# Segment sums of a Mamba-2 scan as split float32r products, and a reordered mixer stage

## What is computed

```
Acs = jnp.cumsum(dtc * A.reshape(G, E), axis=2)
seg = Acs[:, :, :, None] - Acs[:, :, None, :]
Lmat = jnp.exp(jnp.where(causal, seg, -jnp.inf))
y_diag = jnp.einsum('bcign,bcjgn,bcijge,bcjgep->bcigep', CB, Lmat, xdt)
log_a = -LRU_C * r * jax.nn.softplus(-lam)      # r, ig: sigmoids of two small products
u = jnp.sqrt(-jnp.expm1(2.0 * log_a)) * (ig * xf)
_, h = lax.associative_scan(_lin_combine, (jnp.exp(log_a), u), axis=1)
lru_out = rmsnorm(h * jax.nn.gelu(lru_y), lru_out_norm)
```

## Time and profile before

| | before |
|---|---|
| median of 3 runs | 2287.84 us (2287.51 to 2288.26) |
| profiled execution | 2287.8 us, of which the span is 2286.1 us |
| granted clock of TensorE, mean | 0.996 |
| PE busy | 2245.0 us (98%) in 14337 matmul records |
| VectorE, ScalarE, GpSimd busy | 994.8 us (44%), 474.2 us (21%), 745.6 us (33%) |
| chain that ended last | PE 93%, DVE 2%, ACT 2%, DMA 1%, issue 1% |

### The profile page before, as it was taken

How to read it: one execution, slowest core, us unless ns; L and a number is a source line. 1 busy time by engine, 2 the same in 40 slices (tenths; PEclk the granted TensorE clock), 3 DMA queues, 4 the chain that set the end, 5 groups by cost and what they waited for, 6 DMA issues and landing times.

```text
span 2286.1 us, 32012 instructions
## 1 busy us (share of the span) xinstructions
PE 2245.0 (98%) x14337; PEld 2195.3 (96%) x14337; DVE 994.8 (44%) x792; ACT 474.2 (21%) x601; POOL 745.6 (33%) x415
## 2 busy tenths in 40 slices
PE   8999999999999999999999999999999999999997
PEld 8999999999999999988888999999999999999997
DVE  6422122311233557857677586773231123212336
ACT  4100000000002225465564540120000001000102
POOL 4333333333333223432523642323333333333340
PEclk9999999999999999999999999999999999999999
DMA  4111111111112422310111422111111111111112
GB/s 150 47 47 47 47 47 47 47 47 47 47 42 79 130 75 93 121 41 30 49 39 36 170 75 86 47 47 47 47 47 47 47 47 47 46 47 47 47 56 75
DMA packets 48456, 138.35 MB, mean 61 GB/s; under 512 B 7608, under 2 KB 16312, under 8 KB 48320
## 3 DMA queue, kind: packets, MB, share of 16 engines
q1 hardware_dynamic: 47168, 135.78, 18.6%
q10 hardware_dynamic: 1152, 0.52, 0.1%
HBM read 117.67 MB, written 18.79 MB: 60 GB/s over the span
## 4 chain that ended last, share of the span: by engine, by line
PE 93%; DVE 2%; ACT 2%; DMA 1%; issue 1%; ACTq 0%; SPq 0%; POOL 0%; DVEq 0%; POOLq 0%
PE set L572 85%; PE set L807 2%; ACT gate_x L934 1%; PE set L738 1%; PE pair L705 1%; PE set L705 1%; PE pair L713 1%; ACT gate_a L934 1%; PE set L592 0%; PE set L753 0%; PE set L689 0%; PE set L731 0%; PE pair L731 0%; PE pair L735 0%; PE set L735 0%
## 5 line engine op out<-in xcount | busy, mean ns | idle before, releaser
L461 POOL TENSOR_SCALAR w_hi<-w_raw 128x1024 fp32r<-128x1024 f32 (+1 forms) x181 | 193.1, 1067 | 1431.7 <-PE set L572 1230.6
L463 POOL TENSOR_TENSOR w_lo<-w_raw,w_hi 128x1024 fp32r<-128x1024 f32 (+1 forms) x181 | 451.5, 2494 | 27.3 <-issue 0.9
L572 PE MATMUL set<-x_lo,w_hi 128*128 128x344 f32 x2112 | 448.9, 321 | 3.7 <-DVE x_lo L1110 3.7
L572 PE MATMUL set<-x_hi,w_hi 128*128 128x344 f32 x2112 | 449.2, 321 | 1.1 <-ACT x_hi L850 1.1
L572 PE MATMUL set<-x_hi,w_lo 128*128 128x344 f32 x2112 | 446.4, 320 | 0.0
L572 PEld LDWEIGHTS set<-x_lo,w_hi 128*128 128x128 f32 x2112 | 357.8, 189 | 4.6 <-DVE x_lo L1110 4.6
L572 PEld LDWEIGHTS set<-x_hi,w_hi 128*128 128x128 f32 x2112 | 355.7, 188 | 2.2 <-POOL w_lo L470 1.3
L572 PEld LDWEIGHTS set<-x_hi,w_lo 128*128 128x128 f32 x2112 | 352.3, 188 | 0.0
L1106 DVE TENSOR_TENSOR up<-set,rstd 128x1032 f32<-128x1032 f32 x43 | 53.0, 1233 | 419.8 <-PE set L572 419.8
L572 PE MATMUL set<-u_hi,w_hi 128*128 128x344 f32 x864 | 199.1, 339 | 5.4 <-POOL w_lo L463 5.0
L572 PE MATMUL set<-h_hi,w_hi 128*128 128x344 f32 x948 | 201.2, 321 | 0.8 <-DVE h_lo L1130 0.8
(11 more groups left out here) (260 smaller groups left out, 2579.7 us busy)
## 6 DMA issues: line engine op xcount, KB each, us to landing
w_raw<-in_gate_up SPq DMA_DIRECT2D x87, 512.0 KB, 3.5
w_raw<-in_w_in SPq DMA_DIRECT2D x36, 512.0 KB, 4.3
w_raw<-in_down SPq DMA_DIRECT2D x32, 512.0 KB, 3.5
w_raw<-in_w_out SPq DMA_DIRECT2D x16, 512.0 KB, 3.9
w_raw<-in_down SPq DMA_DIRECT2D x16, 384.0 KB, 3.2
x<-in_xt SPq DMA_DIRECT2D x8, 516.0 KB, 8.5
x_kept<-x SPq DMA_DIRECT2D x8, 516.0 KB, 5.0
mixed<-power SPq DMA_DIRECT2D x8, 516.0 KB, 2.9
```

The source lines that it names most:

```text
L461: pool.tensor_scalar(w_hi[s][:, 0:n], w_raw[s][:, 0:n], 1.0, 0.0, ALU.mult, ALU.add)
L463: pool.tensor_tensor(w_lo[s][:, 0:n], w_raw[s][:, 0:n], w_hi[s][:, 0:n].bitcast(F32), ALU.subtract).then_inc(split, 1)
L572: end = pe.matmul(out[:, c, 0:CH], w[s][:, k * P:(k + 1) * P], x[:, kx, c * CH:(c + 1) * CH], start=(first and n == 0), stop=(last and n = ...
```

## The change

- **Segment sums.** In chunks 1 to 7 the product runs in float32r on two terms, `seg_high` and `seg_low`, against a float32r copy `later_r`: four matmuls of 512 columns for each half where there were two in float32. `a` is split once into `a_hi` and `a_lo` (in the storage of `dtw`). ScalarE makes `seg_high` in 16 copies of 128x128 with a scale for each head, at the end of its slot; GpSimd makes `seg_low` in two operations of 1024 columns. Chunk 0 stays as it was.
- **High weights.** ScalarE makes `w_hi` of lx(1) to lx(7); GpSimd makes the low part alone.
- **Waits.** `turn` waits for the first increment of `gate_read` of its slot, which covers `set1`; the second is waited for in `seg(0)`.
- **ScalarE's order.** `btok` comes ahead of the decay terms; both `lmat` exponentials ahead of the root; then the first tap, `e2` and GELU, the high weights and high terms.
- **VectorE's order.** The input of the scan is formed after the second mask; the convolution is in two parts around the first `skip_and_state`. `outputs(1)` stands ahead of tile 2 of ly instead of tile 3.
- **After the slots.** The loads of z2 and z3 are issued ahead of `z_back` and of the prompt state; z2 is scaled ahead of the last scan; the sums "ssd0" and "ssd1" move from z7 to ol2 and from ol3 to ol4, with their roots and reciprocals.

```diff
@@ sync
+            load(("z", EARLY))
+            load(("z", EARLY + 1))
+            sp.wait_ge(state_read, 2 * NCH)
+            for n in range(EARLY):
+                sp.wait_ge(z_stored[n], 16)
+                sp.dma_start(z_back[n][:], d.z_kept[n]).then_inc(z_landed, 16)
+            sp.dma_start(d.prompt_state, ...)
             for t in range(EARLY, KT):
-                load(("z", t))
+                if t >= EARLY + 2:
+                    load(("z", t))
...
@@ gpsimd, split_unit
+                if name[0] == "lx" and name[1]:
+                    pool.wait_ge(lx_high, name[1])
+                else:
...
@@ gpsimd, slots
-                    seg_terms(c + 1)
+                    for g in range(GROUPS):
+                        mine = a_lo[:, c + 1, g * GH:(g + 1) * GH].bitcast(F32)
+                        pool.tensor_tensor(segr_lo[g][:], tri[:].unsqueeze(1).broadcast_to([P, GH, QC]),
+                                           mine.unsqueeze(2).broadcast_to([P, GH, QC]), ALU.mult).then_inc(segr_low, 1)
@@ tensor, turn and seg
-                        pe.wait_ge(gate_read, 2 * c)
+                        pe.wait_ge(gate_read, 2 * c - 1)
...
                         pe.wait_ge(segr_ready, c + 1)
+                        if c:
+                            pe.wait_ge(gate_read, 2 * c)
+                    if c:
+                        pe.wait_ge(segr_low, 2 * c - 1 + g)
...
+                        for low, part in enumerate((segr_hi[:, h:h + 4, :], segr_lo[g][:, 4 * n:4 * n + 4, :])):
+                            end = pe.matmul(to, later_r[:], part.rearrange("p h t -> p (h t)"),
+                                            start=(low == 0), stop=(low == 1))
...
-                products(("ly", c), u_hi, u_lo, {3: lambda: outputs(1)})
+                products(("ly", c), u_hi, u_lo, {2: lambda: outputs(1)})
@@ scalar
+            def seg_terms(c):
+                act.wait_ge(seg_done, 2 * c)
+                act.wait_ge(a_split, 1)
+                for h in range(HEADS):
+                    last = act.activation(segr_hi[:, h, :], tri[:], ACT.Copy, scale=a_hi[:, c, h:h + 1].bitcast(F32))
+                last.then_inc(segr_ready, 1)
...
+                    lru_gelu(c - 1)
+                if c < NCH - 1:
+                    u = U(("lx", c + 1))
+                    act.wait_ge(used, u - 1)
+                    act.wait_ge(landed[u % 2], 16 * (u // 2 + 1))
+                    act.activation(w_hi[u % 2][:], w_raw[u % 2][:], ACT.Copy).then_inc(lx_high, 1)
+                    seg_terms(c + 1)
@@ vector
                 mask(c, 1)
+                if c:
+                    lru_scan_input(c - 1)
+                convolve_first(XT + c, lraw[c % 2], lacc)
                 skip_and_state(c, 0)
-                convolve(XT + c, lraw[c % 2], lacc)
+                convolve_rest(XT + c, lraw[c % 2], lacc)
```

More of the change, by code:

```diff
@@ L134, in make_plan @@
         s = 1 - s
-        if t in (4, 7):
-            p.take(("sum", "lru" if t == 4 else "ssd0"), s)
+        if t == 4:
+            p.take(("sum", "lru"), s)
     for m in range(KT):
@@ L139, in make_plan @@
         s = 1 - s
-        if m == 3:
-            p.take(("sum", "ssd1"), s)
+        if m in (2, 4):
+            p.take(("sum", "ssd0" if m == 2 else "ssd1"), s)
     for m in range(KT):
@@ L230, in build @@
         segr = at("seg_terms", Y, [HEADS, QC])
+        segr_hi = at("seg_high", Y, [HEADS, QC], F32R)
+        segr_lo = [at(f"seg_low{g}", Y + 2 + g, [GH, QC], F32R) for g in range(GROUPS)]
         lmat = [at(f"lmat{g}", Y + 2 + g, [GH, QC]) for g in range(GROUPS)]
@@ L411, in sync @@
                     sp.dma_start(d.mixed[:, 6 if t == 2 else 7, :], sq[:]).then_inc(mixed_stored, 16)
-                if t == 2:
-                    sp.wait_ge(state_read, 2 * NCH)
-                    sp.dma_start(d.prompt_state, ht[:].rearrange("p h c -> p (h c)")).then_inc(outputs_stored, 16)
-                    for n in range(EARLY):
-                        sp.wait_ge(z_stored[n], 16)
-                        sp.dma_start(z_back[n][:], d.z_kept[n]).then_inc(z_landed, 16)
                 if t == 5:
@@ L770, in tensor @@
                     pe.wait_ge(gate_read, 2 * NCH)
-                hooks = {4: {4: lambda: sums("lru", tl, KT - 1)}, 7: {6: lambda: sums("ssd0", t0, 3)}}.get(t)
+                hooks = {4: lambda: sums("lru", tl, KT - 1)} if t == 4 else None
                 products(("z", t), u_hi, u_lo, hooks)
             for m in range(KT):
-                products(("ol", m), l_hi, l_lo, {4: lambda: sums("ssd1", t1, 3)} if m == 3 else None,
-                         l_split if m == 0 else None)
+                hooks = {2: {4: lambda: sums("ssd0", t0, 3)}, 4: {4: lambda: sums("ssd1", t1, 3)}}.get(m)
+                products(("ol", m), l_hi, l_lo, hooks, l_split if m == 0 else None)
             pe.wait_ge(s_split, KT)
@@ L996, in scalar @@
                                    ACT.Exp).then_inc(lmat_exp, 1)
-                    if c and g == 0:
-                        lru_finish(c - 1)
+                if c:
+                    lru_root(c - 1)
+                else:
+                    act.wait_ge(dec_y, KT)
+                freed(("lx", c))
+                first_tap(XT + c, lraw[c % 2], lacc)
                 if c:
@@ L1009, in scalar @@
             lru_decays(NCH - 1)
-            lru_finish(NCH - 1)
+            lru_root(NCH - 1)
+            lru_gelu(NCH - 1)
             def z_tile(t):
@@ L1034, in scalar @@
                     root("lru", tl, 1.0 / DM)
-                if t == 7:
-                    root("ssd0", t0, 2.0 / DM)
                 z_tile(t)
@@ L1203, in vector, with tap, convolve_first, convolve_rest @@
             reciprocal("mix", rstd)
-            def convolve(q, raw, acc):
-                dve.wait_ge(tap0, q + 1)
-                for k in range(HIST):
-                    dve.drain()
-                    n = HIST - k
-                    last = dve.scalar_tensor_tensor(acc[:, n:PROMPT], raw[:, 0:PROMPT - n], pars[:, q, k:k + 1],
-                                                    acc[:, n:PROMPT], ALU.mult, ALU.add)
-                    if k == 0:
-                        dve.tensor_tensor(acc[:, PROMPT:T], acc[:, PROMPT:T], hist_sum[:, q, :], ALU.add)
-                last.then_inc(convolved, 1)
+            def tap(q, raw, acc, k):
+                n = HIST - k
+                dve.drain()
+                return dve.scalar_tensor_tensor(acc[:, n:PROMPT], raw[:, 0:PROMPT - n], pars[:, q, k:k + 1],
+                                                acc[:, n:PROMPT], ALU.mult, ALU.add)
+            def convolve_first(q, raw, acc):
+                dve.wait_ge(tap0, q + 1)
+                tap(q, raw, acc, 0)
+                dve.tensor_tensor(acc[:, PROMPT:T], acc[:, PROMPT:T], hist_sum[:, q, :], ALU.add)
+            def convolve_rest(q, raw, acc):
+                tap(q, raw, acc, 1)
+                tap(q, raw, acc, 2).then_inc(convolved, 1)
+            def convolve(q, raw, acc):
+                convolve_first(q, raw, acc)
+                convolve_rest(q, raw, acc)
             def decode_scale(t):
```

65 lines of the change are left out of this document (38 added, 27 removed).

## The result

The changed kernel takes 2257.05 us (median of four runs, 2256.04 to 2258.64) against 2287.68 us (2286.89 to 2288.26) for the kernel before on the same chip. The ratio is 0.9867, with a 95% interval of 0.985 to 0.9884. Forecast were 2255.1 us and a range of 2250 to 2263 us. The profiled execution took 2256.04 us, 2254.3 us of it span, with a mean granted clock of 0.998.

A forecast was written before the change was run, and what follows sets the result against it. TensorE was taken as the bound, busy nearly the whole span, with waits mostly in the mixer. Terms 10.9 + 10.0 + 5.1 - 0.7 + 7.0 + 0.4 = 32.7 us, from 2287.8 to 2255.1 us; range 2250 to 2263 us.

The forecast's parts named there:

- Segment sums: Chunks 1 to 7: four 512-column float32r matmuls take 0.94 us a half instead of 1.72 us; gain 10.9 us.
- z3: Behind the slots: issuing z3's load half a slot earlier ends its wait and the lower clock; gain 7.0 us.
- ol0: Unit ol0: the root's wait goes, a 1.3 us wait at tiles 6 and 7 comes; net gain 0.4 us.
- The turn: Transposes in each slot: the first increment of the gate reading falls before TensorE arrives, so their wait goes; gain 10.0 us.
- Both exponentials first: First outputs in each slot: the second exponential ends at about 13.6 us, so their wait goes; gain 5.1 us.
- The border: Six slot borders: scan and GpSimd's low part exclude each other, holding lx 0.35 us each; net -0.7 us.
- Rival (1): Slot borders: the scan gets in first, TensorE isn't held and 2.1 us come back; 2253.0 us, chance 0.20.
- (2): Slots: a ScalarE or VectorE chain is 2 us longer, each slot loses 1 to 1.5 us; 2262 to 2266 us, chance 0.17.
- (3): z3 still waits, as the new queue puts its load behind a full buffer; 2262.1 us, chance 0.08.
- (4): Segment sums: float32r at 512 columns is no faster than float32; 2266.0 us, chance 0.04.
- (5): Slots: ScalarE becomes the bound through slow float32r copies; about 2292 us at 0.9 us a copy, chance 0.02.
- (6): ScalarE in the slots: a function-set switch also drains for 1.38 us, making e2 late; 2272.5 us, chance 0.03.

The follow-up runs named there:

- the kernel before with the new queue: Kernel before, with loads of z2 and z3, then z_back, the prompt state and the mixed tiles issued in that order behind the slots: 2279.74 us.

## Why the prediction was right, and where not

The three steps in the slots and z3 went by the mechanism that was walked. The term that failed is ol0, a small gain by the forecast and a loss in the runs; beside it the border came out better than forecast, and the edit named for z3 is not the one that was needed.

**Segment sums**, forecast 10.9 us: 0.92 us a half instead of 0.94 us, and 10.94 us when undone. The row of 344 columns was the right one to scale.

**The turn**, forecast 10.0 us: the wait is gone in all slots. Undone alone it costs 9.5 us. The old trace has a wait of 2.6 us in slot 1 and about 1.06 us in the others; the kernel with the step undone has 1.2 us at the longest.

**Both exponentials first**, forecast 5.1 us: the end at 13.6 us into the slot is as walked, and no wait is left. No run has this step alone in the kernel before; that it gives 5.1 us there is borne out only by the seven slots as a whole (below). Taken out of the changed kernel it costs 33 us (2289.55 - 2256.57, of two comparisons; 31.5 us of it in the slots). The wait for the late exponential stands behind segment sums and turn on TensorE, so it takes up what they give, and the lower clock comes on top, some 1.8 us a slot. The prediction put the three down as a sum, which is right for the whole change. Undone alone, the first two cost about what the sum has for them, and the third over six times as much.

**The border**, forecast -0.7 us (a hold of 0.35 us in each of six borders against 1.4 us of old gaps): this step failed, to the good side. The order is as walked, low part first, then the scan; the halves are done at 30.2 us into the slot (30.4 forecast). But I put 0.2 us between scan and reading that are not there, since the records overlap by 0.1 us (2.28 us from 1076.25, next start 1078.45), and took VectorE for 0.35 us later than TensorE where it is just in time. The sum of the seven slots shows it: 25.3 us forecast, 27.66 measured. Without the 2.1 us of the hold the terms give 27.4. Rival (1) gave this slot, but for a wrong reason: the scan did not get in first.

The sentence on the shared port pair from the Trainium skill's page "SBUF — State Buffer" (Who interferes with whom) holds in the changed trace as well, with a sharper row than those of before: 2.41 us for 8 columns beside a low part of 2.40 us. It has the right mechanism, but at this place it set no price.

**z3**, forecast 7.0 us: 6.95 measured, with a granted clock of 1.00 in z3, and 6.98 us in the kernel before with the new queue. The size is right. The edit that I named for it, z3's load half a slot earlier, is neither enough nor needed: with only that, the gain was 4.75 us; with `z_back` issued early and z3's load behind it, it was all there.

**ol0**, forecast +0.4 us (0 to 1.7): -3.98 us in one profile, -1.8 us in the other. This is the mis-sized term of the sum. The root's wait went as forecast. The new wait at tile 6 was forecast with 1.3 us and measured 4.20 and 2.03 us. I had priced VectorE's last two low parts (3.94 us before, 3.83 us now), and they kept their price. What grew are the three ahead of them, 3.70 us to 6.69 us or 4.49 us, as GpSimd splits ol1 beside them; with ol0 3.4 us earlier the two operations meet. Without that growth (2.99 and 0.79 us) both waits would be 1.2 us, so the rest of the walk holds. And the lower clock behind the wait, some 1.5 us, was not in the term at all, although the prediction had just charged it for z3.

The total is near partly by luck: slots 2.4 us better and a start 1.2 us earlier by chance stand against 4.4 us in ol0. That gives the profiled execution's 2256.04 us for 2255.1 us; the median, 2257.05 us, lies 1.0 us above it.

**The rivals.** (2), a chain 2 us longer, did not come: the high terms and the table load behind them are done at 29.3 us (29.7 forecast). (3), z3 waiting still: no wait. (4), float32r no faster at 512 columns: 0.23 us. (5), ScalarE as the bound: 16 copies in 4.77 us are 0.30 us each, as in the row of eight. (6), a switch of function set: the exponential starts 1062.56 - 1061.26 = 1.30 us after its table load does, again with nothing between. The Trainium skill's page "ScalarE: Activation LUTs" (What ACT_TABLE_LOAD costs) would have 2.66 us there; the trace does not agree.

## What to carry to other kernels

Gains ahead of a wait belong to the wait: before adding terms up, write for each engine the time at which it gets to each meeting point, and take the difference of the two slots, not the sum of the edits. Where an edit ends a wait of 2 to 4 us, or makes one, allow for the lower clock behind it as well, 1.5 to 2.6 us where it came here. Where gains ahead of a wait and a cure of the wait itself are in one kernel, a part that is undone alone shows what it is worth in that kernel, not its share. A move that saves 1.7 us at a place where another engine is nearly late is best tried without it as well: here the kernel without it was faster.
